# One mixed job in place of a full job and a pair job: interleaving two kinds of expert work group by group

## The reference

```
for e in range(8):
    out = out + gate_te[:, e:e + 1] * ((silu(t @ w1[e]) * (t @ w3[e])) @ w2[e])
```

## Time and profile before

| | us |
|---|---|
| median of three runs | 1321.52 |
| profiled execution, device time | 1322.0 |
| its span, first to last instruction | 1320.3 |
| PE busy | 1233.5 |
| VectorE busy | 683.4 |
| ScalarE busy | 565.8 |

### The profile page before, as it was taken

The page is one execution under the profiler, slowest core; times in us unless marked ns, Lnnn a source line. Parts: engine busy times, 40 slices in busy tenths (PEclk is TensorE's granted clock), DMA queues, the critical chain, the costliest instruction groups (busy, mean ns, idle before and its releaser), DMA issues.

```text
span 1320.3 us, 17014 instructions
## 1 busy us (share of the span) xinstructions
PE 1233.5 (93%) x6502; PEld 900.4 (68%) x6502; DVE 683.4 (52%) x793; ACT 565.8 (43%) x578; POOL 17.5 (1%) x54
## 2 busy tenths in 40 slices
PE   9998999999999999999777899999999999997776
PEld 7687999998777778733222588888888888332222
DVE  4946445442454899600000498889889887100002
ACT  2145555542552777400000377767776775000001
POOL 4000000000000000000000000000000000000000
PEclk9998999999999999999999899999999999999999
DMA  9332555571044799799999999989997999899996
GB/s 393 137 152 96 191 173 179 189 281 69 0 192 191 299 338 381 300 405 422 421 421 421 421 421 421 421 351 374 375 374 292 374 379 346 330 421 422 421 421 260
DMA packets 55671, 411.69 MB, mean 312 GB/s; under 512 B 6208, under 2 KB 6336, under 8 KB 7104
## 3 DMA queue, kind: packets, MB, share of 16 engines
q1 hardware_dynamic: 55440, 410.68, 78.0%
q10 hardware_dynamic: 144, 0.26, 0.1%
q0 software_dynamic: 32, 0.00, 0.0%
HBM read 409.87 MB, written 1.05 MB: 311 GB/s over the span
## 4 chain that ended last, share of the span: by engine, by line
PE 75%; SPq 13%; DMA 4%; DVE 3%; ACT 2%; issue 2%; DVEq 0%; ACTq 0%
SPq L474 13%; PE banks L981 11%; PE banks L983 11%; PE banks L982 11%; PE banks L740 10%; PE banks L1003 10%; PE banks L750 5%; DMA raw<-in_exp_dram 4%; PE banks L679 2%; PE banks L642 2%; PE banks L779 2%; PE banks L914 2%; PE banks L831 2%; PE banks L942 1%; DVE low L1506 1%
## 5 line engine op out<-in xcount | busy, mean ns | idle before, releaser
L1506 DVE TENSOR_TENSOR low<-raw,high 128x2048 fp32r<-128x2048 f32 x168 | 383.6, 2289 | 53.0 <-ACT high L1179 50.8
L1179 ACT ACTIVATE high<-raw 128x2048 fp32r<-128x2048 f32 x168 | 321.9, 1919 | 131.7 <-PE banks L983 131.7
L1003 PE MATMUL banks<-raw,x_full 128*64 128x512 f32 x896 | 201.1, 596 | 33.5 <-DMA raw<-in_exp_dram 33.4
L1691 DVE TENSOR_TENSOR prod_h<-banks,gate_h 128x512 f32<-128x512 f32 x42 | 28.8, 686 | 309.8 <-PE banks L1003 309.8
L981 PE MATMUL banks<-high,x_high 128*128 128x512 f32 x448 | 179.0, 399 | 7.2 <-DVE low L1506 5.5
L983 PE MATMUL banks<-high,x_low 128*128 128x512 f32 x448 | 175.7, 392 | 0.0
L982 PE MATMUL banks<-low,x_high 128*128 128x512 f32 x448 | 175.5, 392 | 0.0
L1003 PEld LDWEIGHTS banks<-raw,x_full 128*64 128x64 f32 x896 | 66.8, 137 | 156.9 <-issue 156.8
L1003 PE MATMUL banks<-raw,h_full 128*64 128x512 f32 x448 | 101.0, 595 | 23.1 <-DMA raw<-in_exp_dram 22.4
L1244 ACT ACTIVATE h_full<-banks 128x512 f32<-128x512 f32 x14 | 8.4, 597 | 239.9 <-PE banks L942 239.9
L981 PEld LDWEIGHTS banks<-high,x_high 128*128 128x128 f32 x448 | 84.7, 189 | 27.2 <-DVE low L1506 7.7
(11 more groups left out here) (251 smaller groups left out, 1510.6 us busy)
## 6 DMA issues: line engine op xcount, KB each, us to landing
raw<-in_exp_dram SPq DMA_DIRECT2D x336, 1024.0 KB, 12.7
raw<-in_ff_dram SPq DMA_DIRECT2D x33, 1024.0 KB, 4.7
weights<-in_w_qkv_dram SPq DMA_DIRECT2D x1, 6144.0 KB, 17.1
weights<-in_w_in_conv_dram SPq DMA_DIRECT2D x4, 1024.0 KB, 10.6
weights<-in_w_out_dram SPq DMA_DIRECT2D x2, 2048.0 KB, 25.1
weights<-in_w_o_dram SPq DMA_DIRECT2D x1, 4096.0 KB, 13.9
weights<-in_w_in_pool_dram SPq DMA_DIRECT2D x1, 2048.0 KB, 17.5
natural<-in_x_dram SPq DMA_DIRECT2D x1, 1024.0 KB, 5.8
```

The lines of the kernel that those rows point to most:

```text
L1003: mm = pe.matmul(PS[rows, bank, :], own[:, k, rows], raw[:, raw_slot[(2 * i + t) % UNITS], w], start=first, stop=last)
L1179: act.activation(high[:, i % SPLIT, :], raw[:, raw_slot[i], :], ACT.Copy).then_inc(high_ready, 1)
L1506: dve.tensor_tensor(low[:, i % SPLIT, :], raw[:, raw_slot[i], :], high[:, i % SPLIT, :].bitcast(F32), ALU.subtract).then_inc(low_ready, 1)
L1691: dve.tensor_tensor(prod_h[:, :], PS[:, (1, 3)[g % 2], :], gate_h[:, :], ALU.mult).then_inc(prod_ready, 1)
```

## The change

A pair job no longer runs by itself. FIRST runs, then a mixed job (one full expert and the first pair together), then the loop of full jobs (one here instead of two and one), then a second mixed job. The list `joint` sets the order of the 126 loads of a mixed job, and PE works in the same order: in group g the four full ups, the pair downs of group g-1, the four pair ups, the full downs. The full part has PSUM banks 0, 1, 4, 5 and the pair part 2, 3, 6, 7; each part has one pair of banks for its ups, and its hidden product is transposed into its own first bank. `gate_h` and `prod_h` are shared by both. The pair part has its own selection, x_full, h_full, selT and slot_gate; x_full and h_full move to where they don't overlap the full part's tiles.

The handover moves too. In a full job `gather`, `way_back` and `turn_sel` now stand after the last unit. In a mixed job `gather_pair` stands after the second full unit, and the end has `way_back` between the last two pair units, then `gather`, `way_back_pair` and `turn_sel`. The semaphores of the early stages, one for each of four uses, become one each with counted values. The loop count is written to the table as one number less two.

```diff
+    raw_slot = [(i + 10) % RAW for i in range(3 * UNITS)]
...
+        full_order.append((kind, g, n))
...
+        pair_order.append((kind, g, n))
+        joint.extend([("pair", 2 * len(pair_order) - 2), ("pair", 2 * len(pair_order) - 1)])
...
+            full_part("up", g, n)
+        for n in range(2 if g else 0):
+            pair_part("down", g - 1, n)
+        for n in range(4):
+            pair_part("up", g, n)
+        for n in range(2):
+            full_part("down", g, n)
+    for n in range(2):
+        pair_part("down", GROUPS - 1, n)
...
+        x_full = at("x_full", KEEP_AT + 4 * K8, [P, KD, P])
+        h_full = at("h_full", KEEP_AT + 4 * K8 + (D + 2 * NB * P) * 4, [P, GF, P])
...
+                    if t < RAW:
+                        sp.wait_ge(low_ready, split_before(t - RAW + 1))
                     else:
...
+                        gone, last = joint[t - RAW]
+                        if gone == "full":
+                            sp.wait_ge(low_ready, by_nth(job, UNITS, last + 1))
+                        else:
+                            sp.wait_ge(pair_done, PAIR_UNITS * p + last + 1)
+                    if part == "full":
+                        load_unit(e, stream.index(full_order[m]), raw_slot[t])
+                    else:
+                        load_unit(two[m % 2], stream.index(pair_order[m // 2]), raw_slot[t])
...
+            def gather_pair(job, p):
+                pe.wait_ge(pair_sel_ready, p + 1)
...
+                    if m % 4 == 3:
+                        mm.then_inc(pair_gathered, 1)
...
+            def turn_sel_pair(job, p):
+                pe.wait_ge(back_added, by_nth(job, 4, HEAD))
+                turn(sel_pair, SPARE).then_inc(pair_selT_done, 1)
...
+                gather(following)
+                way_back(job, (T, SPARE, Y, Y + 1))
+                turn_sel(following)
+            def mixed_job(job, p, following):
+                banks = (0, 1, Y, Y + 1)
+                pe.wait_ge(prod_ready, by_nth(job, GROUPS, HEAD))
+                for g in range(GROUPS):
+                    for n in range(4):
+                        full_unit(job, 6 * g + n, ("up", g, n), banks)
+                        if (g, n) == (0, 1):
+                            gather_pair(job, p)
+                        if (g, n) == (0, 3):
+                            turn_sel_pair(job, p)
+                    for n in range(2 if g else 0):
+                        pair_unit(job, p, "down", g - 1, n)
+                    for n in range(4):
+                        pair_unit(job, p, "up", g, n)
+                        if n == 0:
+                            pe.wait_ge(prod_ready, by_nth(job, GROUPS, HEAD + g + 1))
+                            turn_prod(0).then_inc(turned, 1)
+                    for n in range(2):
+                        full_unit(job, 6 * g + 4 + n, ("down", g, n), banks)
+                    pe.wait_ge(pair_prod_ready, GROUPS * p + g + 1)
+                    turn_prod(2).then_inc(pair_turned, 1)
+                pair_unit(job, p, "down", GROUPS - 1, 0)
+                way_back(job, (0, 1, Y, Y + 1))
+                pair_unit(job, p, "down", GROUPS - 1, 1)
+                if following:
+                    gather(following)
+                pe.wait_ge(back_added, by_nth(job, 4, HEAD + 4))
+                way_back_pair(p, (6, 7, Y, Y + 1))
+                if following:
...
+                split_next(following, 0)
+                take_out(job)
                 for half in range(2):
                     take_tokens(following, half)
...
+                    split_next(following, i)
...
+            def mixed_job(job, p, following):
+                for g in range(GROUPS):
+                    if g:
+                        act.wait_ge(pair_turned, GROUPS * p + g)
+                        act.activation(h_full[:, :, :], PS[:, 2, :].rearrange("p (f n) -> p f n", n=P), ACT.Copy
+                                       ).then_inc(pair_h_ready, 1)
+                    split_mixed(job, 6 * g + 3)
+                    act.wait_ge(unit_done, by_nth(job, UNITS, SPLIT + 6 * g + 2))
+                    if g:
+                        act.wait_ge(pair_prod_ready, GROUPS * p + g)
+                    else:
+                        act.wait_ge(prod_ready, by_nth(job, GROUPS, HEAD))
+                        act.wait_ge(back_done, by_nth(job, 4, HEAD))
+                    act.activation(gate_h[:, :], PS[:, 0, :], ACT.Silu).then_inc(gate_ready, 1)
+                    if g == 0:
+                        for half in range(2):
+                            act.wait_ge(pair_gathered, 2 * p + half + 1)
+                            act.activation(x_full[:, 4 * half:4 * half + 4, :],
+                                           PS[:, 2 + half, :].rearrange("p (k n) -> p k n", n=P), ACT.Copy
+                                           ).then_inc(pair_x_ready, 1)
+                    take_hidden(job, g, 0)
+                    act.wait_ge(pair_done, pairs_done(p, "up", g, 1))
+                    act.wait_ge(prod_ready, by_nth(job, GROUPS, HEAD + g + 1))
+                    act.activation(gate_h[:, :], PS[:, 2, :], ACT.Silu).then_inc(pair_gate_ready, 1)
+                    for k in range(6 * g + 4, min(6 * g + 9, UNITS)):
+                        split_mixed(job, k)
+                act.wait_ge(pair_turned, GROUPS * p + GROUPS)
+                act.activation(h_full[:, :, :], PS[:, 2, :].rearrange("p (f n) -> p f n", n=P), ACT.Copy
+                               ).then_inc(pair_h_ready, 1)
                 take_out(job)
...
+                split_low(following, 0)
+                take_out(job)
+                take_tokens(following, 0)
+                split_low(following, 1)
+                take_tokens(following, 1)
+                split_low(following, 2)
+                add_back(job, (6, 7, 4, 5))
+                take_sel(following, expert)
...
+            def mixed_job(job, p, following, at, offset):
+                experts = pair_of(p)
+                select_pair(experts)
+                for g in range(GROUPS):
+                    split_mixed(job, 6 * g + 3)
+                    if g:
+                        dve.wait_ge(pair_turned, GROUPS * p + g)
+                    dve.wait_ge(unit_done, by_nth(job, UNITS, SPLIT + 6 * g + 4))
+                    take_prod(job, g, 1)
+                    if g == 0:
+                        take_sel_pair(p, experts)
+                        if following:
+                            expert = single(at)
+                            select(expert, offset)
+                    take_hidden(job, g, 0)
+                    split_mixed(job, 6 * g + 4)
+                    dve.wait_ge(pair_gate_ready, GROUPS * p + g + 1)
+                    dve.wait_ge(pair_done, pairs_done(p, "up", g, 3))
+                    dve.tensor_tensor(prod_h[:, :], PS[:, 3, :], gate_h[:, :], ALU.mult).then_inc(pair_prod_ready, 1)
+                    for k in range(6 * g + 5, min(6 * g + 9, UNITS)):
+                        split_mixed(job, k)
+                take_out(job)
+                add_back(job, (0, 1, 4, 5))
+                take_out_pair(p)
+                if following:
+                    take_tokens(following, 0)
                     split_low(following, 0)
...
+                    take_tokens(following, 1)
                     split_low(following, 1)
...
+                add_back_pair(p, (6, 7, 4, 5))
+                if following:
+                    take_sel(following, expert)
```

More of the change, by code:

```diff
@@ L502, in _ @@
                 for i in range(UNITS):
+                    split = i - RAW + 1
                     if i < RAW:
-                        sp.wait_ge(pair_done, PAIR_UNITS - RAW + i + 1)
-                    sp.wait_ge(low_ready, UNITS * j + (UNITS + i - RAW + 1))
+                        gone = joint[len(joint) - RAW:len(joint) - RAW + i + 1]
+                        sp.wait_ge(pair_done, max(m for part, m in gone if part == "pair") + 1)
+                        split = max([split] + [m + 1 - UNITS for part, m in gone if part == "full"])
@@ L907, in _, with gather @@
             H1, Y, T, SPARE = (0, 2), 4, 6, 7
-            def gather(job, half):
-                pe.wait_ge(sel_ready, by_seq(job, 1, 1))
-                for m in range(4 * half, 4 * half + 4):
+            def gather(job):
+                pe.wait_ge(sel_ready, by_nth(job, 1, 1))
+                for m in range(KD):
                     for b in range(NB):
@@ new lines, in turn @@
+            def turn(chosen, bank):
+                for b in range(NB):
+                    pe.transpose(PS[:, bank, b * P:(b + 1) * P], chosen[:, b, :], ident[:, :])
+                for b in range(NB):
+                    mm = pe.matmul(PS[:, bank, NB * P:NB * P + NE], chosen[:, b, :], gates[:, b, :],
+                                   start=(b == 0), stop=(b == NB - 1))
+                return mm
+            def turn_sel(job):
+                pe.wait_ge(x_high_ready, by_nth(job, 2, 1))
```

(8 more changed lines are left out.)

541 lines of the change are left out of this document (259 added, 282 removed).

## The result

The changed kernel takes 1318.31 us (median of 20 runs, 1315.77 to 1321.03) where the kernel before takes 1321.4 (20 runs beside them, 1319.83 to 1321.97): a ratio of 0.9979, interval 0.9972 to 0.9986. It is faster, by 0.2%, not by the 0.6% forecast: 5 us of the 8 are missing.

What follows compares the result with a forecast made beforehand. PE bounds full jobs and the weight stream pair jobs; mixed jobs would be bound by DMA. Sum: 550.5 + 301.8 + 138.4 + 301.8 + 8.1 + 10.9 + 1.7 = 1313.2 us, against 1322.0 profiled; range 1302 to 1327.

Steps and rivals of the forecast that it cites:

- The stream at 421 GB/s: Mixed jobs: weight loads by DMA set the length, 44.8 us a group against 38.8 for PE.
- the ring: The 14 load slots inside a mixed job: always freed in time, tightest margin 4.3 us, so no idling there.
- Rival 4: Inside mixed groups, loads behind the pair-down slots lack free slots: 2 us in 12 groups, 24 us, 1337; chance 0.16.
- The wait of unit 40 for h_low: End of a full job before a mixed one: unit 40 waits for h_low, which ends at 544.87.
- the pair's selection: Mixed job's start: VectorE makes it after splits and add backs, leaving PE idle 3.1 us ahead of gather_pair.
- E: End of the last full unit before a mixed job; first forecast at 550.5 us.
- the handover: From a mixed job's last pair unit through the loop's full job to the next E: 130.3 us.
- the tail: From the last pair unit to the kernel's end: 10.9 us, as before.
- Rival 3: Idle PE at mixed starts and handover halves the clock: three places, 2.7 us each, 1321, no difference; chance 0.13.
- A: Landing of a mixed job's last load; its last pair unit was forecast to end 8.1 us later.
- Rivals 1 and 2: Mixed starts 3.5 to 5 us cheaper each, 1303 to 1306, chance 0.10; stream never idles, 1270, chance 0.05.
- The restart: Stream resuming at a mixed job's start after the first pair unit, landing latency included: 4.3 us, bounds 1.5 to 5.1.

Runs made afterwards that it cites:

- half loads: Changed kernel with the mixed jobs' pair loads bringing only the first half of their columns, output wrong, all matmuls and waits kept: 1273.47 us (one run).
- the early selections: Changed kernel with both pair selections made long before and take_sel ahead of the third split and add backs on VectorE: 1309.39 us, ratio 0.9918.

## Why the prediction was wrong

**Right: the bound and its shape.** The stream at 421 GB/s sets the length of the mixed jobs (half loads: 1273; idle matmuls in the fourth group: no cost), the ring never runs dry in a group, and the loop's full job hides all its loads. Rival 4 would have shown under 410 GB/s. The wait of unit 40 for h_low, the pair's selection (done at E + 14.6, forecast E + 15.0), the handover (130.6 against 130.3) and the tail (11.1 against 10.9) came as written.

**Wrong: the term of the clock at the starts and ends.** My sum had E + 25.3 for the start of the first pair unit and 281.0 from there to the last one, 306.3 in all. At full clock the runs show 24.4 + 281.8 = 306.2 (a gather starts some 0.2 before E): right to 0.1 us. With the clock lost at both places they show 26.1 + 283.4 = 309.5. The step that failed is thus PE's work behind the waits at the two edges of a mixed job, which the sum priced at full clock: it cost 3.3 us more in each job (1.7 at the start, 1.6 at the end), 6.6 of the 7.2 us missed in the stage. With idle matmuls at both places the kernel takes 1313.63 us, and 1313.2 was forecast.

That the rest comes out to 0.1 us is partly luck: at full clock the start is 0.8 us shorter than in the sum (the wait 2.6 instead of 3.1 among it) and the restart 0.8 longer, and where the load of the second full down landed late, 24.4 + 282.4 = 306.8 is the sum.

**Rival 3 had the mechanism, but neither its places nor its price.** I gave it 0.13, three places, 2.7 us each. Its places were the mixed starts and the handover. At the starts a loss is 1.6 to 1.7 us. I overlooked the ends: PE waits 3.1 us for the last downs' low splits there. My sum had those splits (low done at A - 8.1), but the rival left out the idle time that they mean. The same wait stands from the fourth group of a mixed job on (in the first three PE doesn't wait there): 2.4 to 3.1 us in the six inner groups of the first profile, with the clock lost in three of them. Slack covers both there; in the last group they end on the chain. At the handover the clock fell as well, and cost nothing in the profiled run. Of the changed kernel, windows there and PE at the loop job's units 0 and 2:

```profile
872.00:875.00 3.00, 3.00 (x8) 2.32 (x7) 3.00 (x5) 0.14 (x1) 0.00 (x0) 0.50 1.03 429
```
```profile
870.46 0.50 PE L1040 MATMUL banks<-high,x_high 128*128 128x512 f32 x1 [2.39 <-DVE low L1627]
878.24 0.50 PE L1040 MATMUL banks<-high,x_high 128*128 128x512 f32 x1 [0.43 <-DVE low L1627]
```

And with idle matmuls at the ends alone, where it fell one wait later:

```profile
868.06 0.50 PE L1040 MATMUL banks<-high,x_high 128*128 128x512 f32 x1 [2.39 <-DVE low L1629]
875.85 0.50 PE L1040 MATMUL banks<-high,x_high 128*128 128x512 f32 x1 [1.98 <-DVE low L1629]
```
```profile
878.00:881.00 3.00, 3.00 (x10) 2.36 (x9) 2.71 (x3) 0.64 (x1) 0.00 (x0) 0.59 1.01 418
```

In the first case slow matmuls only shorten the next wait, from 1.98 to 0.43 us; unit 2 starts 7.8 us after unit 0 in both. In the second no wait follows, and the same stretch to the next gather took 132.1 us instead of 130.5. These 1.6 us would more than account for the 0.9 by which the run missed the 1315 expected.

The Trainium skill (TensorE: Matmul & The Clock Gate, "HAM oscillation") says that waits for data between bursts of matmuls throttle the engine again and again; I held 1.3 us of idle time in every 4.97 at full clock against it. The trace agrees with both: 1.3 us cost no clock. Of the twelve starts and ends of the changed kernel's three profiles eleven have waits of 2.6 to 3.1 us, and ten of these lost it. Only what stands on the chain behind such a wait is paid for.

**Rivals 1 and 2**: the start is 0.8 us cheaper than my sum at full clock, not 3.5 to 5, and two gaps remain. **The restart** is 5.1 us instead of 4.3, by the landing of the last load (852.2, worked out from the start of ScalarE's copies for the last full downs, 839.76 and 842.25, as in the sum): 852.2 - 578.5 - 108 x 2.487 = 5.1. The 2 us that the prediction took from the Trainium skill (DMA: Bandwidth & Descriptors, "Anatomy of one DMA") lie further off; that section is on DMAs issued by GpSimd, and SyncE issues the loads here.

## What to carry to other kernels

In a job bound by a stream through a ring, count PE's work only between the last release of a slot ahead of the gap and the first one behind it, and behind the last landing; price a wait like those here (2.4 to 3.1 us) twice, once as itself and once, at the odds seen here (8 of the 11 such waits in the mixed and loop jobs of the first profile), as the 1.6 to 1.7 us that the matmuls behind it lose at half clock. The first group and the last group of a loop need a sum of their own: what slack covers in the middle is paid for at the edges. Better than idle matmuls is to take away the wait (the early selections: 9 us for a few moved lines). Before moving a unit, ask where its inputs stand in the other engines' queues.

## What the runs showed of the hardware

- The same wait of 2.60 to 2.63 us ahead of the same instruction left the clock at 1.00 in one place of one run and took it to half in another (3.84 and 5.46 us for the same 32 records). A sum can only give it a chance.
- A fall costs nothing where PE would wait next anyway: the next wait shrank from 1.98 to 0.43 us at the handover, and to 1.60 us ahead of last downs that otherwise wait 3.0.
- 13 idle matmuls (26 records, 3.17 us) in a wait of 3.0 to 3.1 us held the clock at the last downs in all four ends of the two profiles with idle matmuls as their only edit. Whether fewer would do was not tried.
- The stage ahead of the experts, with the same instructions, differs by 1.8 us between profiles. What makes it differ stays open.
